# One weight load of 1 MB issued as sixteen loads of eight partitions each

## The chip, the cores and the metric

The kernel runs on one core of one Trainium2 chip. The metric is the device time of one execution in microseconds (us). A core has a matrix engine (PE, with weight loads PEld), a vector engine (DVE), a scalar engine (ACT), GpSimd (POOL), a sequencer that here only issues transfers (SP), and 16 DMA engines that carry the transfers of all of them.

## The reference

Two blocks follow one another on a sequence of 256 tokens with 1024 features, all in float32.

The first block is attention over chosen keys beside a short convolution, and then a feed-forward layer made of 16,384 small experts. Each token has 8 heads; each head picks 16 experts; and the layer is the sum over all these picks:

```
u_sel = peer_u[expert]
a = jax.nn.gelu(jnp.einsum('bqhkd,bqd->bqhk', u_sel, hb))
v_sel = peer_v[expert]
return jnp.einsum('bqhk,bqhkd->bqd', g * a, v_sel)
```

The second block has two layers, each with its own weights `w_in_2`, `w_branch_attn_2`, `w_branch_gmlp_2` and `w_out_2`: a projection into nine parts, sliding-window attention, a gated unit, two branch projections, an output projection, and a layer norm.

## The kernel before, in words

The instructions of each engine are written out by hand, with semaphores between them. Four parts of it matter here.

**The expert stage.** Tokens stand in 128 partitions, in two tiles. For tile, head and pick (2 x 8 x 16 = 256 times) POOL issues one indirect transfer, a gather (L901): each of 128 partitions gets the 8 KB row of its own expert (1024 features of `peer_u`, 1024 of `peer_v`), 1 MB in all. Gather n goes to slot n modulo 12; six slots lie in the tile `rows`, six in `low_pairs`. Before it issues gather n, POOL waits until PE has used gather n - 12 (`pair_used`). When a gather has landed, DVE takes the dot product (L2063), ACT the GELU (L1140), DVE the weight (L2070), ACT builds a diagonal matrix (L1145), and PE adds the pick to the sum with eight products (L1569). ACT and PE do this for four picks at a time.

**The weight ring.** Weights come in units of 128 partitions x 8 KB (1 MB). The tile `wring` has four places. Units 0 to 30 belong to the first block, unit 31 (`N1`) is the first of 2 x 27 units of the second block's layers. Each is split by ACT (`layer_hi`, L704) and DVE (`layer_lo`, L710) into a rounded part and a rest before PE uses it.

**The order of SP.** SP issues all weight loads from one queue. After the last load of the first block it waits for the expert scores (L807, L808), and then runs the loop of L813 to L845. For unit 31 nothing more is waited for: it is issued at once, while the expert stage is under way. For the next one (L816, L817) SP waits until gather 253 has landed, and for the one after that until gather 255, the last, has landed (L820). Each load adds 16 to the semaphore of its ring place, `w_loaded[s]`, and the readers wait for 16 times the number of loads of that place (`w_wait`, L606).

**The first use.** ACT reads unit 31 within the last group of picks: `layer_hi(act, 0, 0)` at L1153, after a pick among the last, and pieces 1 to 3 soon after it.

The transfers of SP and ACT are of the kind `hardware_dynamic` in the profile, those of POOL `software_dynamic`.

Of the kernel before, what the change touches and what calls it, by code (L numbers as in the profile page):

```python
# [22 lines left out]
P = 128  # L23
# [16 lines left out]
RING = 4  # L40
# [60 lines left out]
N1, N2 = len(UNITS_1), len(UNITS_2)  # L101
# [29 lines left out]
def own_group(n):  # L131

    return [n in group for group in OWN_GROUPS].index(True)
# [17 lines left out]
def ada_place(n):  # L151

    if n < 2 * KC:
        return n % FIRST_RING, n // FIRST_RING, n - FIRST_RING if n >= FIRST_RING else None
    place, turn = (n - 2 * KC) % ADA_RING, (n - 2 * KC) // ADA_RING
    return place, 2 * KC // FIRST_RING + turn, n - (ADA_RING if turn else FIRST_RING)


def raw_turn(n):

    return n - sum(own < n for own in OWN_UNITS)
# [87 lines left out]
def use(name, i=0):  # L249

    return [n for n, z in enumerate(USES) if z.name == name][i]
# [64 lines left out]
def build(nc, a, out):  # L316
    ctx = ExitStack()
    with ctx:
        def sb(name, shape, dt=F32):
            return ctx.enter_context(nc.sbuf_tensor(name, shape, dt))  # L320

        def sem(name):
            return ctx.enter_context(nc.semaphore(name))


        wring = sb("wring", [P, RING, WUNIT])
# [63 lines left out]
        spread = ytok.rearrange("p n f -> p (n f)")[0:NT * HEADS, :]  # L390
# [16 lines left out]
        w2 = Area(work[:, :])  # L407
# [81 lines left out]
        w_loaded, own_loaded = [sem(f"w_loaded{s}") for s in range(RING)], [sem(f"own_loaded{s}") for s in range(len(OWN_GROUPS))]  # L489
# [46 lines left out]
            sem("routed"), sem("gate_exp"), sem("dotted"), sem("dots_act"), sem("weighted"), sem("diag_ready"))  # L536
        pair_loaded = [sem(f"pair_loaded{s}") for s in range(SLOTS)]
        pair_used = sem("pair_used")
        x_ready = sem("x_ready")
        bias_iota, bias_lin, bias_ready = sem("bias_iota"), sem("bias_lin"), sem("bias_ready")  # L540
        vn_ready, vn_std, vn_stat = sem("vn_ready"), sem("vn_std"), sem("vn_stat")
# [23 lines left out]
        def chunk_out(m, width=T):  # L565
            b, j, _, _ = SEATS_1[m]
            z = aux[:, 3 + b, :] if b < BATCH else pj[:, b % 2, :]
            return z[:, j * T:j * T + width]
# [23 lines left out]
        def bank_free(pe, m):  # L592
# [3 lines left out]
            if j == 0 and b >= BATCH + 2:  # L596
                last = SEATS_1[first - 1][2]
                who = OWN_1[last - 1]
                pe.wait_ge({"a": taken_act, "d": taken_dve}[who], OWN_1[:last].count(who))

        def w_wait(eng, n):

            if n in OWN_UNITS:
                eng.wait_ge(own_loaded[own_group(n)], 16 * len(OWN_GROUPS[own_group(n)]))
            else:
                eng.wait_ge(w_loaded[raw_turn(n) % RING], 16 * (raw_turn(n) // RING + 1))  # L606

        def w_slot(n):
            width, chunks = UNITS_1[n][2:] if n < N1 else (256, KC)
# [19 lines left out]
        def split_hi(act, n):  # L629

            if PIECES_1[n].column == 0:
                w_wait(act, PIECES_1[n].unit)

            before = [k for k, z in enumerate(PIECES_1) if z.place <= PIECES_1[n].place - PRING]
            if before:
                act.wait_ge(proj, DONE_1[before[-1]])
            nc.scalar.copy(parts(n)[0], piece_of_unit(n)).then_inc(w_hi, 1)
# [23 lines left out]
        def wait_emptied(eng, l, u):  # L661

            who = USES[u].owner
            eng.wait_ge(emptied[who], l * EMPTIES[who] + sum(z.owner == who for z in USES[:u + 1]))
# [26 lines left out]
        def layer_hi(act, l, *pieces):  # L691

            for p in pieces:
                unit = N1 + l * N2 + p // 2
                if p % 2 == 0:
                    w_wait(act, unit)
                r = ring_place(l, p)
                if r is not None and r >= PRING:
                    was, q = RING_ORDER[r - PRING]
                    act.wait_ge(steps, was * STEPS + PIECE_DONE[q])  # L700
                if r is None:
                    act.wait_ge(steps, l * STEPS + FILLED[use("bg", 3)])
                    act.wait_ge(y_split, l * 2 + 2)
                nc.scalar.copy(layer_part("hi", l, p), layer_raw(l, p)).then_inc(w_hi, 1)  # L704
# [7 lines left out]
        def wait_lo(eng, l, p):  # L712

            eng.wait_ge(w_lo["d"], LO_1.count("d") + SPLIT_ORDER.index((l, p)) + 1)
# [45 lines left out]
        def _(sp):  # L760
# [3 lines left out]
            def load_ada(n):  # L764
                place, turn, was = ada_place(n)
                if was is not None:
                    sp.wait_ge(ada_used, was + 1)
                sp.dma_start(ada[:, place, :], a["w_ada"][ada_column(n)]).then_inc(ada_loaded[place], 16)
# [41 lines left out]
            def load_rows(dst, name, l, done):  # L810
                sp.dma_start(dst, a[name][l:l + 1].partition_broadcast(P).rearrange("p o d -> p (o d)")).then_inc(done, 16)

            for l in range(LAYERS):  # L813
                for n in range(N2):
                    unit = N1 + l * N2 + n
                    if l == 0 and n == 1:  # L816
                        sp.wait_ge(pair_loaded[(LAST_PICK - 2) % SLOTS], 16 * ((LAST_PICK - 2) // SLOTS + 1))  # L817
                    if l == 0 and n == 2:
                        load_rows(vg_rows.rearrange("p l f -> p (l f)"), "vg_rows", 0, vg_rows_loaded)
                        sp.wait_ge(pair_loaded[LAST_PICK % SLOTS], 16 * (LAST_PICK // SLOTS + 1))  # L820
                    if l == 0 and n == 4:
                        sp.wait_ge(routed, NT * EXPERT_HEADS)
                        sp.wait_ge(gate_exp, NT * EXPERT_HEADS)
                        load_rows(late_rows, "late_rows", 0, late_rows_loaded)
                    if l == 0 and n == 6:
                        load_rows(brow.rearrange("p l n -> p (l n)"), "brow", 0, brow_loaded)
                    if n == 10:
                        if l == 0:
                            sp.wait_ge(x0_turned, 2 * NT)
                        else:  # L830
                            wait_emptied(sp, l - 1, use("gg", 3))
                        load_rows(gate_rows, "gate_rows", l, gate_rows_loaded)
                    if n == 17:
                        sp.wait_ge(att2["summed"], l * NT + NT)
                        load_rows(norm_rows, "norm_rows", l, norm_rows_loaded)
                        if l + 1 < LAYERS:
                            sp.wait_ge(x0_taken, 2 * NT)
                            sp.wait_ge(vn_ready, l * NT + NT)
                            load_rows(late_rows, "late_rows", l + 1, late_rows_loaded)
                    if unit - RING >= N1:  # L840
                        was, q = divmod(unit - RING - N1, N2)
                        wait_lo(sp, was, 2 * q)
                        wait_lo(sp, was, 2 * q + 1)
                    s = raw_turn(unit) % RING
                    sp.dma_start(wring[:, s, :], a["w2"][l, n]).then_inc(w_loaded[s], 16)  # L845
            for t in range(NT):
                for c in range(2):
                    sp.wait_ge(x_normed, (LAYERS - 1) * 2 * NT + 2 * t + c + 1)
# [424 lines left out]
        def _(pe):  # L1273
# [83 lines left out]
            def first_products(k, n):  # L1357

                pe.wait_ge(h_ready, k + 1)
                w_wait(pe, n)  # L1360
                w, m = w_slot(n), 2 * n
                for j in range(1 if n == 2 else 2):
                    ins = mm(chunk_out(m + j), w[:, k, j * P:(j + 1) * P], hT[:, k, :], start=(k == 0 and j == 0), stop=(k == KC - 1),  # L1363
                             skip_group_check=True)
                    if k == KC - 1 and n < 2:
                        ins.then_inc(proj, 1)
                if n == 2:
                    for t in range(NT):
                        ins = mm(chunk_out(m + 1)[:, t * HEADS:(t + 1) * HEADS], hT[:, k, tile_of(t)], w[:, k, P:P + HEADS], start=False, stop=(k == KC - 1),
                                 skip_group_check=True)  # L1370
                    if k == KC - 1:
                        ins.then_inc(proj, 2)
# [377 lines left out]
        def _(dve):  # L1750
# [3 lines left out]
            def ada_dots(lo, hi):  # L1754

                for n in range(lo, hi):
                    place, turn, _ = ada_place(n)
                    dve.wait_ge(ada_loaded[place], 16 * (turn + 1))
                    tile = ada[:, place, :]
                    v.tensor_tensor_reduce(tile, tile, cbc, 1.0, 0.0, ALU.mult, ALU.add,  # L1760
                                           mod[:, ada_column(n):ada_column(n) + 1]).then_inc(ada_used, 1)
# [622 lines left out]
```

## Time and profile before

| what | value |
|---|---|
| median of three runs | 1176.72 us (1174.97 to 1177.11) |
| the profiled execution, its own time | 1175.45 us |
| its span | 1173.5 us |
| PE, PEld, DVE, ACT, POOL busy | 90%, 84%, 71%, 37%, 23% of the span |
| moved by DMA | 390.35 MB, 333 GB/s over the span |
| of it gathers | 268.45 MB |

The span is cut into 40 slices of 29.3 us in the page's second part. The expert stage takes slices 6 to 28; there the row of GB/s stands at 419 to 422 almost without a break, and after it at 160 to 230.

### The profile page before, as it was taken

How to read it: one execution, taken by the hardware profiler on the slowest of the kernel's cores; microseconds unless marked ns; L12 is line 12 of the kernel's file. 1: busy time of each engine (PE TensorE's matmuls, PEld its weight loads, DVE VectorE, ACT ScalarE, POOL GpSimd, SP SyncE). 2: the span in 40 equal slices, each digit the busy share in tenths (PEclk: the TensorE clock that was granted, in tenths of full speed). 3: DMA queues.
4: the chain of work that ended last, by engine and by line, in shares of the span. 5: the costliest groups of instructions: out<-in, count | busy, mean ns of one | idle time of the engine just before them, and what ended most of it. 6: DMA issues, size and time to landing. Idle time of an engine off the chain costs nothing.

```text
span 1173.5 us, 18891 instructions
## 1 busy us (share of the span) xinstructions
PE 1052.4 (90%) x7587; PEld 982.2 (84%) x7587; DVE 836.9 (71%) x1801; ACT 432.9 (37%) x913; POOL 269.0 (23%) x289
## 2 busy tenths in 40 slices
PE   8999997999999888887777878778999999999997
PEld 6999986998899878887777878778899888898885
DVE  6999987568566667666776766656765868775776
ACT  3646832123212221222122122212557554476452
POOL 2001004334334333333333333434000000300000
PEclk9999998999999998899898998999999999999999
DMA  9986858999999999999999999999855655455540
GB/s 371 406 330 224 350 189 350 419 421 419 422 419 421 420 421 421 420 421 420 421 420 420 421 421 421 421 421 421 348 185 177 232 198 180 157 202 180 193 166 36
DMA packets 59576, 390.35 MB, mean 333 GB/s; under 512 B 6881, under 2 KB 7905, under 8 KB 15714
## 3 DMA queue, kind: packets, MB, share of 16 engines
q0 software_dynamic: 36864, 268.45, 55.1%
q1 hardware_dynamic: 21152, 120.10, 27.5%
q8 instruction: 60, 0.98, 0.3%
q10 hardware_dynamic: 1474, 0.60, 0.2%
q14 instruction: 26, 0.21, 0.0%
HBM read 388.08 MB, written 1.05 MB: 332 GB/s over the span
## 4 chain that ended last, share of the span: by engine, by line
PE 60%; DMA 26%; DVE 7%; ACT 4%; issue 1%; SPq 0%; DVEq 0%; ACTq 0%
DMA rows<-in_peer_uv,work 25%; PE aux L1569 22%; PE pj L1612 5%; PE pj L1614 5%; PE pj L1613 5%; PE pj L1289 5%; PE pj L1290 5%; PE pj L1291 5%; PE aux L1548 4%; DVE rows L2063 2%; DMA rows<-in_w_ada 1%; PE aux L1363 1%; ACT work L1145 1%; ACT rows L1013 1%; PE aux L1428 1%
## 5 line engine op out<-in xcount | busy, mean ns | idle before, releaser
L1569 PE MATMUL aux<-work,rows 128*128 128x128 f32 x2080 | 262.9, 291 | 70.7 <-ACT work L1145 70.7
L1569 PEld LDWEIGHTS aux<-work,rows 128*128 128x128 f32 x2080 | 256.1, 206 | 78.2 <-ACT work L1145 78.0
L1569 PE MATMUL aux<-work,low_pairs 128*128 128x128 f32 x2016 | 239.7, 280 | 30.5 <-ACT work L1145 30.3
L1569 PEld LDWEIGHTS aux<-work,low_pairs 128*128 128x128 f32 x2016 | 234.6, 196 | 34.1 <-ACT work L1145 34.1
L901 POOL DMA_INDIRECT rows<-in_peer_uv,work x130 | 122.4, 942 | 296.0 <-PE aux L1569 229.6
L710 DVE TENSOR_TENSOR wlo<-wring,whi 128x1024 fp32r<-128x1024 f32 x100 | 121.0, 1235 | 77.7 <-ACT whi L704 77.1
L901 POOL DMA_INDIRECT low_pairs<-in_peer_uv,work x126 | 118.2, 938 | 160.5 <-PE aux L1569 155.8
L1289 PE MATMUL pj<-xh,whi 128*128 128x256 f32 x512 | 146.4, 286 | 0.2
L1140 ACT ACTIVATE work<-work 128x4 f32<-128x4 f32 (+2 forms) x71 | 14.7, 207 | 357.1 <-DVE work L2063 357.1
L1290 PE MATMUL pj<-xl,whi 128*128 128x256 f32 x512 | 144.8, 283 | 0.0
L1291 PE MATMUL pj<-xh,wlo 128*128 128x256 f32 x512 | 144.8, 283 | 0.0
L2063 DVE CUSTOM_DVE_ANT_0 low_pairs<-low_pairs,aux 128x1024 f32<-128x1024 f32 x64 | 77.6, 1220 | 54.2 <-DMA low_pairs<-in_peer_uv,work 54.1
L704 ACT CAST whi<-wring 128x1024 fp32r<-128x1024 f32 x100 | 102.2, 1050 | 24.7 <-PE pj L1614 23.3
L2063 DVE CUSTOM_DVE_ANT_0 rows<-rows,aux 128x1024 f32<-128x1024 f32 x64 | 77.0, 1218 | 39.3 <-DMA rows<-in_peer_uv,work 39.2
L1289 PEld LDWEIGHTS pj<-xh,whi 128*128 128x128 f32 x512 | 98.1, 192 | 2.6 <-issue 1.8
L1290 PEld LDWEIGHTS pj<-xl,whi 128*128 128x128 f32 x512 | 98.2, 192 | 0.0
L1291 PEld LDWEIGHTS pj<-xh,wlo 128*128 128x128 f32 x512 | 98.2, 192 | 0.0
L1145 ACT ACTIVATE work<-ident,work 128x128 f32<-128x128 f32 x256 | 82.6, 390 | 21.5 <-DVE work L2070 21.5
L2063 DVE CUSTOM_DVE_ANT_0 rows<-rows,pj 128x1024 f32<-128x1024 f32 x66 | 78.1, 1217 | 16.7 <-DMA rows<-in_peer_uv,work 16.3
L2063 DVE CUSTOM_DVE_ANT_0 low_pairs<-low_pairs,pj 128x1024 f32<-128x1024 f32 x62 | 73.6, 1218 | 22.5 <-DMA low_pairs<-in_peer_uv,work 22.2
L1612 PE MATMUL pj<-whi,xh 128*128 128x512 f32 x192 | 76.0, 396 | 1.7 <-DVE xl L2077 1.3
L1614 PE MATMUL pj<-wlo,xh 128*128 128x512 f32 x192 | 74.9, 390 | 0.0
(288 smaller groups left out, 1464.4 us busy)
## 6 DMA issues: line engine op xcount, KB each, us to landing
wring<-in_w SPq DMA_DIRECT2D x76, 1024.0 KB, 4.8
rows<-in_w_ada SPq DMA_DIRECT2D x46, 512.0 KB, 9.2
rows<-in_w SPq DMA_DIRECT2D x3, 1024.0 KB, 11.2
rows<-in_peer_uv,work POOLq DMA_INDIRECT x130, 17.3
work<-in_late_rows SPq DMA_DIRECT2D x2, 1024.0 KB, 7.6
xT<-in_gate_rows SPq DMA_DIRECT2D x2, 1024.0 KB, 7.5
rows<-in_norm_rows SPq DMA_DIRECT2D x2, 1024.0 KB, 7.5
low_pairs<-in_peer_uv,work POOLq DMA_INDIRECT x126, 17.9
```

The source lines that it names most:

```text
L704: nc.scalar.copy(layer_part("hi", l, p), layer_raw(l, p)).then_inc(w_hi, 1)
L710: dve.tensor_tensor(layer_part("lo", l, p), layer_raw(l, p), full(layer_part("hi", l, p)), ALU.subtract).then_inc(w_lo["d"], 1)
L901: pool.indirect_dma_start(out=pair(n), out_offset=None, in_=a["peer_uv"], in_offset=bass.IndirectOffsetOnAxis(ap=expert[g % EXPERTS][:, j: ...
L1145: nc.scalar.activation(diag[:, j, :], ident[:, :], ACT.Copy, scale=weight[g % 2][:, j:j + 1]).then_inc(diag_ready, 1)
L1289: mm(o, w[0], x[0], start=start, stop=False, skip_group_check=skip)
L1290: mm(o, w[0], x[1], start=False, stop=False, skip_group_check=skip)
L1291: return mm(o, w[1], x[0], start=False, stop=stop, skip_group_check=skip)
L1569: ins = mm(peer_sum[t][:, c * P:(c + 1) * P], pair(n)[:, D + c * P:D + (c + 1) * P], diag[:, n % PICKS, :], start=(n % (EXPERT_HEADS * PIC ...
L1612: mm(bank(u), hi[:, k, ts], w_hi_[:, j, :], start=(k == 0), stop=False)
L1613: mm(bank(u), lo[:, k, ts], w_hi_[:, j, :], start=False, stop=False)
L1614: ins = mm(bank(u), hi[:, k, ts], w_lo_[:, j, :], start=False, stop=(k == last))
L2063: v.tensor_tensor_reduce(row, row, h2_tok[g // EXPERT_HEADS], 1.0, 0.0, ALU.mult, ALU.add, dots[g % 2][:, j:j + 1]).then_inc(dotted, 1)
```

## The change

Unit 31 is loaded by sixteen transfers in place of one. Transfer i carries partitions 8i to 8i + 7 (`SPREAD_ROWS` = 8), 64 KB, and adds 16 to a semaphore of its own, `spread_loaded`. The readers of unit 31 wait for 256 there. The later loads of the same ring place count one load fewer. All other loads are as before, and so are their order and the waits ahead of them.

```
+SPREAD_UNIT, SPREAD_ROWS = N1, 8
...
+        def loads_till(n):
+
+            spread = raw_turn(n) % RING == raw_turn(SPREAD_UNIT) % RING and raw_turn(n) > raw_turn(SPREAD_UNIT)
+            return raw_turn(n) // RING + 1 - spread
+
         def w_wait(eng, n):
...
+            elif n == SPREAD_UNIT:
+                eng.wait_ge(spread_loaded, 16 * (P // SPREAD_ROWS))
             else:
-                eng.wait_ge(w_loaded[raw_turn(n) % RING], 16 * (raw_turn(n) // RING + 1))
+                eng.wait_ge(w_loaded[raw_turn(n) % RING], 16 * loads_till(n))
...
                     s = raw_turn(unit) % RING
-                    sp.dma_start(wring[:, s, :], a["w2"][l, n]).then_inc(w_loaded[s], 16)
+                    if unit == SPREAD_UNIT:
+                        for at in range(0, P, SPREAD_ROWS):
+                            rows_ = slice(at, at + SPREAD_ROWS)
+                            sp.dma_start(wring[rows_, s, :], a["w2"][l, n][rows_, :]).then_inc(spread_loaded, 16)
+                    else:
+                        sp.dma_start(wring[:, s, :], a["w2"][l, n]).then_inc(w_loaded[s], 16)
```

## Rows read from the trace of the kernel before

**Rows 1.** Busy time by stretch: us, engines' busy (instructions), PEclk, DMA share, GB/s.
```profile
177.00:190.00 13.00, 12.44 (x62) 10.84 (x63) 5.11 (x23) 3.61 (x8) 7.51 (x7) 1.00 0.76 286
...
230.00:393.00 163.00, 152.05 (x1224) 146.43 (x1222) 110.91 (x282) 40.16 (x108) 62.42 (x67) 1.00 1.01 420
393.00:403.00 10.00, 8.53 (x77) 8.49 (x77) 8.75 (x29) 6.42 (x15) 3.97 (x5) 1.00 1.01 420
403.00:813.00 410.00, 329.06 (x2637) 321.64 (x2636) 273.35 (x656) 87.01 (x239) 153.31 (x166) 0.93 1.01 421
```

**Rows 2.** Chain that ended last, 751 to 835 us: start, us, what.
```profile
751.34 20.84 DMA rows<-in_peer_uv,work
...
774.42 7.42 PE aux L1569 x64
781.85 0.26 issue
782.11 19.91 DMA rows<-in_peer_uv,work
...
811.94 21.13 DMA rows<-in_peer_uv,work
833.07 0.02 issue
833.09 1.22 DVE rows L2063
```

**Rows 3.** SP's waits, 400 to 850 us: us in total, times, longest.
```profile
SPq L845 <- DMA rows<-in_peer_uv,work: 438.5, 2, 433.4
```

**Rows 4.** SP in order of time: start, us, instruction.
```profile
393.13 0.33 SPq L845 DMA_DIRECT2D wring<-in_w  x1
...
826.84 0.33 SPq L845 DMA_DIRECT2D wring<-in_w  x1
827.21 0.74 SPq L811 DMA_DIRECT2D pq<-in_vg_rows  x1
833.09 0.80 SPq L845 DMA_DIRECT2D wring<-in_w  x2
```

**Rows 5.** Instructions on wring, 820 to 850 us: ns min/median/max, first and last start.
```profile
L704 ACT CAST whi<-wring x7: 1028/1034/1055, 822.2 to 849.3; 128x1024 fp32r<-128x1024 f32 x7
```

**Rows 6.** DMA issues of 388 to 394 us: KB each, us to landing.
```profile
wring<-in_w SPq DMA_DIRECT2D x1, 1024.0 KB, 10.3
```

**Rows 7.** DMA queues of the whole span: packets, MB, share of 16 engines.
```profile
q0 software_dynamic: 36864, 268.45, 55.1%
...
q10 hardware_dynamic: 1474, 0.60, 0.2%
```

**Rows 8.** DMA issues of ACT in the whole span: KB each, us to landing.
```profile
wsT<-in_wsT ACTq DMA_DIRECT2D x1, 512.0 KB, 20.0
...
cols<-in_cols ACTq DMA_DIRECT2D x1, 45.0 KB, 5.4
lcol<-in_lcol ACTq DMA_DIRECT2D x1, 18.0 KB, 23.0
rows<-in_c ACTq DMA_DIRECT2D x1, 4.0 KB
sink<-in_sink ACTq DMA_DIRECT2D x1, 8.0 KB, 21.4
```

**Rows 9.** Busy time by stretch at the end of the expert stage, columns as above.
```profile
820.00:822.00 2.00, 1.86 (x17) 1.67 (x16) 1.65 (x5) 0.69 (x3) 0.00 (x0) 1.00 0.96 397
822.00:824.00 2.00, 2.00 (x21) 2.00 (x20) 1.73 (x4) 1.71 (x4) 0.00 (x0) 1.00 0.73 307
824.00:826.00 2.00, 2.00 (x21) 2.00 (x20) 1.92 (x3) 0.13 (x2) 0.00 (x0) 1.00 0.56 233
```

**Rows 10.** DMA queues, 393 to 827 us: packets, MB, share of 16 engines.
```profile
q8 instruction: 22, 0.36, 0.3%
q14 instruction: 10, 0.08, 0.0%
```

More of the change, by code:

```diff
@@ L538, in build @@
         pair_used = sem("pair_used")
+        spread_loaded = sem("spread_loaded")
         x_ready = sem("x_ready")
```

## The prediction

> **What bounds the kernel now.** I read the table of stretches first, then the chain of waits, then SP's own waits and issues, and last the DMA queues. The change touches one load, so the question is what runs beside it and whether that is on the path to the end.
>
> The load is issued at 393.13 us [rows 4]. In the stretches around it all sixteen DMA engines are full: a share of 1.01 at 420 GB/s from 230 to 393 us, during the load, and from 403 to 813 us at 421 GB/s, while PE is busy for 329 of 410 us (80%) and DVE for 67% [rows 1]. No compute engine is full there, the transfers are. At the start of the expert stage that was not yet so, 0.76 from 177 to 190 us [rows 1]. The chain of waits says the same: it goes round a loop of a gather that takes 20 to 21 us to land, some 2.4 us on DVE and ACT, 7.42 us of PE (64 products, eight picks), 0.26 us, and the next gather [rows 2]. From landing to landing (772.18 us, from 751.34 + 20.84, to 802.02, from 782.11 + 19.91) that is 29.8 us for the twelve gathers of the twelve slots, 2.49 us each; and 1.05 MB at 421 GB/s is 2.49 us. So the DMA engines set the pace of this stage, and a microsecond of extra work on the engine that is last is a microsecond at its end.
>
> The end of the stage is on the path as well. The last gather lands at 833.07 us; DVE takes it at 833.09 [rows 2] and SP issues the next weight units at 833.09 [rows 4], so the second block moves with it.
>
> **The change part by part.** The sums are made in the profiled execution (1175.45 us, span 1173.5 us, so 1.95 us lie around it); it is 1.27 us below the median of 1176.72 us, and I add the change to the median.
>
> *Issue on SP.* Fifteen more issues of 0.33 us; two in a row take 0.80 us [rows 4], so about 0.4 us each, 6 us in all. Behind them in SP's queue stands a wait of 433.4 us for gather 253 [rows 3]. Cost nothing; it would cost from a 434th microsecond on.
>
> *Wait of the readers.* The unit is first read at 822.2 us [rows 5], 429 us after its issue; it landed after 10.3 us [rows 6]. Even a landing four times slower is hidden. The new semaphore and the count of the later loads cost nothing: the number of wait instructions is the same.
>
> *Bytes.* The same 1 MB. As one transfer over 16 engines it is 64 KB for each, eight rows of 8 KB. An engine moves 421 / 16 = 26.3 GB/s, so a row takes 0.311 us and the load takes 2.49 us from every engine. That cost is in the time before.
>
> *Which engines.* No row shows a plain transfer of eight partitions. The nearest is the one of a single row: ACT's load of `c`, 4 KB [rows 8]. Queue q10 holds ACT's transfers, 1474 packets [rows 7]. Three loads of 128 partitions (`cols`, `lcol`, `sink`) are 384 packets, `wsT` is 8 pieces x 128 = 1024, and `c` as one piece is 1: 1409. The other 65 are 4 x 16 + 1, a closing packet for each engine that took part: sixteen for each of the four wide loads, a single one for `c`. The gathers agree: 36864 packets are 256 x (128 + 16) [rows 7]. So a transfer of one row ran on one engine, and I take it that one of eight rows runs on eight. If these are the same eight each time, each gets 16 rows, 4.98 us, and the other eight none. Bounds: nothing (if the sixteen transfers take turns over all engines) and 8 x 0.311 = +2.49 us on eight engines. I take +2.49, because it is nearest to the row of `c`.
>
> The Trainium skill says so outright in "DMA: Bandwidth & Descriptors", section "Why a DMA increments its semaphore by 16 and not by 1": the number of engines is the largest up to 16 that divides the outer sizes, and for transfers issued by SP or ACT they are the lowest-numbered ones. By it eight rows go to the same eight engines each time; the one closing packet of `c` agrees, and which eight they are no row here shows.
>
> *Whether the eight get in each other's way.* In the wide load and in every gather each engine has its own eight partitions. In a small transfer eight engines write to eight neighbouring partitions at the same moment. If neighbours share a way into the memory, a packet there takes longer, and its engine can't go on with its gather in that time. No row shows this. Lower bound: 0.311 us for a row as ever, nothing more. Upper bound: four engines at one place from beginning to end, so a row takes 4 x 0.311 and each of sixteen transfers costs 3 x 0.311 = 0.93 us more, 14.9 us in all. Between packets of the small transfers each engine has a gather packet, which goes to its own place, so the engines fall out of step and the four seldom meet in full. I take two at a time: 16 x 0.311 = +4.98 us. Both ends are kept for the range.
>
> *Slack.* The engines are not level. The last gather is issued at 811.94 us and its last part lands at 833.07 [rows 2], yet the share of the DMA engines falls to 0.96, 0.73 and 0.56 from 820 to 826 us [rows 9]: some have finished all their gathers while others have seven microseconds to go. What else the engines carry can unlevel them: 22 + 10 packets of instructions fall between 393 and 827 us [rows 10], and not evenly, I suppose. A lag on an engine that is ahead is free as far as its lead goes. Up to 826 us the idle time is 2 x (0.04 + 0.27 + 0.44) = 1.5 us per engine on the mean; the bounds are 0 (the last engine is one of the eight) and about 12 us (the first to finish, 821 against 833). I take -1.5.
>
> *The sum.* 2.49 + 4.98 - 1.5 = +6.0 us: 1181.4 us for the profiled execution, 1182.7 us for the median.
>
> **The rivals.**
>
> *In step.* The four engines at one place stay together for all sixteen transfers: 2.49 + 14.9 = +17.4, with the slack +15.9 us, 1192.6 us. For it: SP issues every 0.4 us, so all eight engines find their row at the same time. Against it: the gather packets between them, as above. The Trainium skill, "SBUF — State Buffer", section "Door 1: The DMA port swizzle (why `[64,N]` ≈ `[32,N]`)", speaks for it: four neighbouring partitions lie on one of 16 ports, so eight reach two, and a load into one port ran at 27.6 GB/s. As an estimate from that page, 64 KB over two ports would be 1.2 us and all sixteen 19 us, against 5 us without sharing. No run here shows it so far.
>
> *Eight engines and no more.* The rows don't hinder one another, and the slowest engine is one of the eight: +2.49 us, 1179.2 us. For it the row of `c`; against it only that neighbours have never been written together in this trace.
>
> *No change.* The sixteen transfers take turns over all engines, or the eight have a lead of over 2.5 us at the end: 0 to +1 us, 1176.7 us. For it: the share of 0.56 at 824 to 826 us says that many engines have such a lead. Against it: with the hold-up the lead would have to be 7.5 us.
>
> *Faster.* The slowest engine, the one that lands last at 833.07 us, is among the eight that get nothing of unit 31. It is then relieved of eight rows, -2.49 us, 1174.2 us. This decides only if the eight that get the rows lag by less than their lead, so with a hold-up of nearly nothing. For it: it is one half or the other; against it: as the gain grows to the full 2.49 us, another engine becomes the last.
>
> That the change does not do what it says would need the unit to land after 822 us or a reader to wait elsewhere; the 429 us above leave no room for it.
>
> **How the numbers follow.** Hold-up of about the assumed size (+3.5 to +10 us): 0.45. In step (+10 to +20): 0.15. Eight engines alone (+1 to +3.5): 0.15. No change: 0.17. Faster: 0.08. The bound of what can be told from no change is 0.2%, 2.35 us. Slower by more than it are the first two and about half of the third, 0.67; faster by more than it is a part of the last, and I give it 0.08 with what a measurement scatters; within it the rest, 0.25. The range goes from 1175.5 us, which holds the cases of no change and leaves out most of the faster one, to 1190 us, which leaves out the upper part of the case in step.
>
> **What would show it.** In the profile after, SP issues sixteen transfers from about 393 us on, about 0.4 us apart. Queue q1 has 16 x (8 + 8) = 256 packets for the unit in place of 144, 112 more; 16 x (8 + 16) = 384, so 240 more, would say that every small transfer closes on all engines and that they are spread wider. The share of the DMA engines, or the GB/s, falls below 421 within some 20 us after 393 us if there is a hold-up: 6 us of lost time on eight engines is a dip to about 300 GB/s over 10 us. It stays level where the engines only carry more. The stage's last gather lands at 839 us in place of 833, and the second block keeps its length of 340 us. From 820 us to the last landing there is more idle time, because the other eight engines finish about 2.5 us earlier against the rest. The forecast is wrong if the last landing moves by less than 3 us, or if it moves and the second block gives it back.

## The result, and the profile after

The kernel after takes 1191.63 us (four runs, 1191.26 to 1192.53), the kernel before 1175.93 us (four runs). The ratio is 1.0135, with a 95% interval of 1.0123 to 1.0147: slower by some 15.9 us. The forecast was 1182.7 us, in a range of 1175.5 to 1190. The span of the profiled execution grew from 1173.5 to 1189.7 us, by 16.2 us.

The table of stretches around the load, kernel after (us, busy time of PE, PEld, DVE, ACT and POOL with their instructions, granted PE clock, DMA share, GB/s):

```profile
230.00:393.00 163.00, 151.54 (x1219) 145.88 (x1217) 110.53 (x280) 40.64 (x109) 62.49 (x67) 1.00 1.01 421
393.00:398.00 5.00, 4.04 (x36) 4.04 (x37) 4.71 (x9) 4.46 (x10) 0.94 (x1) 1.00 1.02 357
398.00:403.00 5.00, 5.00 (x48) 5.00 (x47) 3.50 (x20) 1.49 (x5) 2.81 (x3) 1.00 1.03 228
403.00:408.00 5.00, 5.00 (x47) 5.00 (x46) 0.54 (x2) 0.00 (x0) 2.00 (x3) 1.00 1.00 215
408.00:413.00 5.00, 1.40 (x13) 1.20 (x11) 1.23 (x2) 0.00 (x0) 1.76 (x2) 1.00 1.04 202
413.00:418.00 5.00, 0.00 (x0) 0.00 (x0) 0.13 (x1) 0.00 (x0) 0.00 (x0) 0.55 1.04 205
418.00:423.00 5.00, 0.00 (x0) 0.00 (x0) 1.10 (x2) 0.00 (x0) 0.00 (x0) 0.50 1.03 200
423.00:428.00 5.00, 0.89 (x4) 0.89 (x5) 2.76 (x9) 1.48 (x5) 0.00 (x0) 0.50 0.94 352
...
453.00:813.00 360.00, 283.29 (x2297) 276.43 (x2296) 242.88 (x595) 77.22 (x212) 134.63 (x144) 0.95 1.01 420
```

Before, this stretch was level at 420 GB/s [rows 1]. Now the same sixteen engines are as busy as ever (share 1.00 to 1.04) and move half as much, for close to 30 us. PE runs out of picks and stands still from 413 to 423 us. After 428 us all is as before. The bytes that were not moved can be added up: (64 + 193 + 206 + 219 + 216 + 221 + 69) GB/s x 5 us are 5.9 MB, which is 14.1 us at 421 GB/s. I call this the lost throughput of a run; below it is worked out for each kernel in the same way. It is a loss of all sixteen engines together: eight engines that stood still for 14 us would lose half of it.

The chain that ended last, kernel after (start, us, what), around the load and at the end of the stage:

```profile
391.61 0.26 issue
391.87 33.00 DMA rows<-in_peer_uv,work
...
427.11 9.04 PE aux L1585 x64
...
436.41 19.24 DMA rows<-in_peer_uv,work
...
828.13 21.07 DMA rows<-in_peer_uv,work
```

The same gather, and the one that follows it, in the chain of the kernel before:

```profile
392.42 16.16 DMA rows<-in_peer_uv,work
...
418.50 20.83 DMA rows<-in_peer_uv,work
```

It takes 33.0 us to land in place of 16.16. The eight picks on PE behind it take 9.04 us in place of 7.42 [rows 2], because PE starts them at a granted clock of 0.50 (1.2 GHz) after its idle time. That adds nothing: the next gather of the chain lands at 455.65 us (436.41 + 19.24) against 439.33 before (418.50 + 20.83), 16.3 us late, as the one before it (424.87 against 408.58). The last gather lands at 849.20 us (828.13 + 21.07) in place of 833.07 [rows 2]: 16.1 us. From there to the end of the span it is 340.5 us, before 340.4. So the whole loss lies in these 30 us, and the second block gave nothing back and lost nothing.

SP's issues, and the queues from 393 to 425 us (packets, MB, share of 16 engines), kernel after:

```profile
392.59 5.41 SPq L859 DMA_DIRECT2D wring<-in_w  x16
```

```profile
q0 software_dynamic: 887, 6.46, 87.3%
q1 hardware_dynamic: 256, 1.05, 13.8%
```

In the kernel before the same 32 us have these rows:

```profile
q0 software_dynamic: 1698, 12.35, 92.9%
q1 hardware_dynamic: 144, 1.05, 7.9%
```

The unit takes 256 packets, 16 x (8 + 8), and not 16 x (8 + 16): a transfer of eight rows runs on eight engines. Issue takes 0.34 us each (5.41 / 16) and nobody waits for it; behind it SP waits 445.0 us for gather 253. What changed is the time of a packet: those of the gathers went from 92.9% x 512 / 1698 = 0.28 us to 87.3% x 512 / 887 = 0.50 us on the mean (closing packets included). The trace also records each packet by itself, though not its engine. A gather packet of 8 KB takes 0.309 to 0.321 us as a rule; in the kernel after, 98% of the 523 that start between 398 and 423 us take over 0.335 us, 0.644 in the median. Eight engines that nothing held would have brought at least half of these packets, in the usual time. So the gathers of all sixteen engines are held up, and not only those of the eight that bring the small rows.

### The profile page after: what moved, and what is told of

The parts are those of the page before. It is cut to its first block, busy times and chain, and to the rows that moved or that the text cites. A ratio compares the mean times of both kernels' runs of the same rounds, so it can differ in the third digit from the quotient of the medians.

```text
span 1189.7 us, 18906 instructions
## 1 busy us (share of the span) xinstructions
PE 1047.9 (88%) x7587; PEld 977.4 (82%) x7587; DVE 836.8 (70%) x1801; ACT 433.0 (36%) x913; POOL 270.1 (23%) x289
## 4 chain that ended last, share of the span: by engine, by line
PE 59%; DMA 28%; DVE 7%; ACT 4%; issue 1%; SPq 0%; DVEq 0%; ACTq 0%
DMA rows<-in_peer_uv,work 26%; PE aux L1585 21%; PE pj L1628 5%; PE pj L1630 5%; PE pj L1629 5%; PE pj L1305 5%; PE pj L1306 4%; PE pj L1307 4%; PE aux L1564 4%; DVE rows L2079 2%; DMA rows<-in_w_ada 1%; PE aux L1379 1%; ACT work L1161 1%; ACT rows L1029 1%; PE aux L1444 1%
## 5 line engine op out<-in xcount | busy, mean ns | idle before, releaser
L1585 PE MATMUL aux<-work,rows 128*128 128x128 f32 x2080 | 256.0, 286 | 88.2 <-ACT work L1161 88.2
L1585 PEld LDWEIGHTS aux<-work,rows 128*128 128x128 f32 x2080 | 249.0, 201 | 95.9 <-ACT work L1161 95.7
L1585 PE MATMUL aux<-work,low_pairs 128*128 128x128 f32 x2016 | 242.5, 282 | 33.4 <-ACT work L1161 33.3
L1585 PEld LDWEIGHTS aux<-work,low_pairs 128*128 128x128 f32 x2016 | 237.4, 198 | 37.1 <-ACT work L1161 37.1
```

The source lines that it names most:

```text
L1585: ins = mm(peer_sum[t][:, c * P:(c + 1) * P], pair(n)[:, D + c * P:D + (c + 1) * P], diag[:, n % PICKS, :], start=(n % (EXPERT_HEADS * PIC ...
```

## The experiments

The theories at the start: *shared places* (neighbouring partitions share a way into the memory, and their rows wait for one another; such a way in, with the partitions behind it, is called a place below), *number of transfers* (each small one costs something, wherever it writes), *half the engines*, and shared places on the *source* side. All kernels are measured against the kernel before.

### Every fourth partition

```
-                        for at in range(0, P, SPREAD_ROWS):
-                            rows_ = slice(at, at + SPREAD_ROWS)
-                            sp.dma_start(...)
+                        for at in range(0, P, 4 * SPREAD_ROWS):
+                            for j in range(4):
+                                rows_ = slice(at + j, at + 4 * SPREAD_ROWS, 4)
+                                sp.dma_start(...)
```

> Still sixteen transfers of eight rows on eight engines, but each takes every fourth partition (0, 4, ... 28, then 1, 5, ... 29, and so on), in the source as in the ring. Shared places (eight neighbours have two ways into the memory, the rows wait for one another): no two of the eight meet, the dip to 205 GB/s for some 30 us goes away, and what is left is the eight extra rows on eight engines, -2.5 to +2.5 us against before: 1173.5 to 1178.5 us. Number of transfers (each small transfer costs the DMA engines about a microsecond, wherever it writes): 1191 us as with the change. Eight engines carry the load of sixteen and that alone: at most +2.5 us, and it could not have made +16 in the first place.

Measured: ratio 1.0049 (1.0035 to 1.0062), +5.8 us. Number, size and engine count of the transfers are those of the change, and nearly two thirds of its cost are gone. But it is more than the 2.5 us that shared places allowed. The stretches of this kernel show where the rest is:

```profile
393.00:398.00 5.00, 3.52 (x32) 3.36 (x31) 4.04 (x9) 4.46 (x10) 1.42 (x2) 1.00 1.01 421
398.00:403.00 5.00, 5.00 (x48) 5.00 (x47) 4.69 (x22) 1.97 (x6) 2.54 (x3) 1.00 1.02 419
403.00:408.00 5.00, 5.00 (x47) 5.00 (x46) 2.39 (x6) 0.00 (x0) 2.13 (x3) 1.00 1.01 323
408.00:413.00 5.00, 2.07 (x19) 1.88 (x17) 1.47 (x4) 0.21 (x1) 1.88 (x2) 1.00 1.03 306
413.00:418.00 5.00, 4.53 (x26) 4.53 (x27) 3.84 (x12) 1.28 (x4) 0.94 (x1) 0.68 1.00 388
```

The first half (partitions 0 to 63) loses nothing, the second half falls to 306 GB/s: (98 + 115 + 33) x 5 / 421 = 2.9 us lost, and with 2.5 us for eight rows more on eight engines 5.4 us.

### The upper half first

The same with `for at in (64, 96, 0, 32)`.

> The run of every fourth partition lost nothing while partitions 0 to 63 were written and fell to some 310 GB/s for ten microseconds while 64 to 127 were. Here the upper half goes first. If the upper partitions are the places of the eight engines that get no row of the small transfers (guests and owners share them), the dip comes at once, from about 395 us, and the second part is level: 1180.5 us again. If the dip came from having many transfers queued, it stays in the second part.

Measured: ratio 1.0050 (1.0035 to 1.0066), +5.9 us. The dip moved to the front:

```profile
393.00:398.00 5.00, 4.29 (x38) 4.29 (x39) 4.95 (x10) 4.25 (x8) 1.11 (x2) 1.00 1.03 387
398.00:403.00 5.00, 5.00 (x47) 5.00 (x47) 3.80 (x19) 1.48 (x5) 2.63 (x3) 1.00 1.02 295
403.00:408.00 5.00, 5.00 (x48) 5.00 (x47) 1.23 (x2) 0.00 (x0) 2.25 (x3) 1.00 1.00 328
408.00:413.00 5.00, 1.14 (x11) 0.95 (x9) 1.71 (x3) 0.00 (x0) 1.50 (x2) 0.98 1.01 416
```

So it belongs to partitions 64 to 127 and not to the time or to a full queue. Lost in these four stretches: (34 + 126 + 93 + 5) x 5 / 421 = 3.1 us. The simplest reading: the same eight engines bring all sixteen transfers, their gathers write the lower half, and in the upper half they meet the gathers of the other eight. That engine and half belong together is inferred from this dip, no row names an engine.

### Sixteen neighbours, thirty-two neighbours

`SPREAD_ROWS` = 16 and 32: eight and four transfers, sixteen engines in each.

> Eight transfers of sixteen neighbouring partitions. All sixteen engines take part, one row each. Shared places: sixteen rows have four ways in, so four engines still meet in each; eight transfers cost 3 x 0.311 us each on all engines, +7.5 us, about 1183.5 us. Engine count (half the engines): nothing is left, 1176 us. Number of transfers: half of +16, 1184 us, which only the run by columns tells from the first.

> Four transfers of 32 neighbouring partitions, two rows for each of sixteen engines. Thirty-two neighbours have eight places, so two engines meet in each: 4 transfers x 2 rows x 0.311 us = +2.5 us, and up to twice that with the owners of the places, 1177.5 to 1180 us. If the price went by the number of transfers and the rows in each alone, a quarter of the change's: +4 us, 1179 us. If sixteen engines in use were enough to be rid of it: 1175 us.

Measured: 1.0074 (1.0060 to 1.0087), +8.7 us, and 1.0033 (1.0023 to 1.0044), +3.9 us. With sixteen engines in use the loss is still there, so *half the engines* is not the cause of the dip (it is that of the 2.5 us of uneven rows, see below). In the sixteen-row kernel the rate is as low as in the change, for half as long:

```profile
398.00:403.00 5.00, 5.00 (x48) 5.00 (x47) 3.12 (x19) 1.60 (x6) 2.81 (x3) 1.00 1.03 202
403.00:408.00 5.00, 5.00 (x48) 5.00 (x47) 1.23 (x2) 0.00 (x0) 1.87 (x2) 1.00 1.07 220
```

### By columns

```
+                        for at in range(0, WUNIT, WUNIT // 16):
+                            part_ = slice(at, at + WUNIT // 16)
+                            sp.dma_start(wring[:, s, part_], a["w2"][l, n][:, part_]).then_inc(spread_loaded, 16)
```

> Sixteen transfers as well, but each over all 128 partitions, 512 bytes of each row. Shared places: every engine writes its own partitions as in the gathers, no dip; 0 to +2 us for the shorter pieces, 1176 to 1178 us. Number of transfers: 1191 us.

Measured: 1.0013 (1.0004 to 1.0022), +1.5 us. Sixteen transfers of 64 KB cost next to nothing if each covers all partitions, even cut into pieces of 512 bytes. SP takes 21.3 us to issue these sixteen, against 5.4 in the change, so they come in more thinly; the run apart in time, below, shows that thinness alone does not help, and the run with sixteen more rows has sixteen small transfers and no dip. *Number of transfers* falls. The lowest rate from 398 to 428 us is this:

```profile
413.00:418.00 5.00, 5.00 (x47) 5.00 (x46) 2.79 (x5) 0.00 (x0) 2.81 (x3) 1.00 1.00 399
```

### Source rows apart

```
+                            rows_, block_ = slice(at, at + SPREAD_ROWS), at // 32 * 32 + at // SPREAD_ROWS % 4
+                            from_ = slice(block_, block_ + 4 * SPREAD_ROWS - 3, 4)
+                            sp.dma_start(wring[rows_, s, :], a["w2"][l, n][from_, :]).then_inc(spread_loaded, 16)
```

> Sixteen transfers of eight neighbouring partitions of the ring, as in the change, but the eight rows are read four rows apart in DRAM (unit 31 is then loaded with its rows in another order, so what follows is computed from other weights). Shared places on the side of the ring: 1191 us, as with the change. Shared places on the side of DRAM (eight rows that follow one another are read from one 64 KB piece): 1174 to 1179 us.

Measured: 1.0152 (1.0136 to 1.0169), +17.9 us, the same as the change within the intervals. Reading the rows apart does not help by itself; every fourth partition, where they are written apart as well, does. The *source side* falls.

### Each transfer by itself, beside the gathers

```
+                            rows_, gather = slice(at, at + SPREAD_ROWS), 86 + 3 * (at // SPREAD_ROWS)
+                            if at:
+                                sp.wait_ge(pair_loaded[gather % SLOTS], 16 * (gather // SLOTS + 1))
```

> The change's sixteen transfers of eight neighbours, but each is issued three gathers (7.5 us) after the one before, so they never meet one another. Hold-up inside each transfer: every one still holds its eight engines for 3 x 0.311 us or more, and the loss stays near +15 us, 1190 us, in sixteen small dips. Hold-up by the queue of transfers (they overtake one another or pile up): most of it goes, 1178 us.

Measured: 1.0149 (1.0134 to 1.0165), +17.5 us. The transfers do not need one another to cost what they cost. The dip is only thinner and longer (the first of the sixteen falls into the first line):

```profile
396.00:401.00 5.00, 4.37 (x39) 4.37 (x40) 4.87 (x10) 4.31 (x9) 1.19 (x2) 1.00 1.02 354
401.00:413.00 12.00, 12.00 (x110) 12.00 (x109) 10.09 (x35) 2.91 (x10) 6.09 (x7) 1.00 1.01 420
413.00:533.00 120.00, 90.81 (x684) 88.90 (x683) 70.91 (x169) 23.77 (x62) 39.61 (x43) 0.89 1.01 377
```

The packets show who pays. Within some 3 us of each of the sixteen transfers, 33 to 48 gather packets take over 0.335 us (the longest of each 0.86 to 1.23 us), while 91 of the 128 rows of the small transfers stay below 0.335. What these gather packets take beyond the usual time is 11 to 17 us of engine time per transfer, 14.2 on the mean, 0.89 us for each of sixteen engines. Eight engines held for 3 x 0.311 us would be 7.5.

### The same loads with the DMA engines idle

The kernel before, and behind the last weight load 1 MB five times into a free place of the ring, each after the last has landed (`load_alone` issues its list and waits for it):

```
+            load_alone(0, [slice(0, P)])
+            load_alone(1, [slice(at, at + 8) for at in range(0, P, 8)])
+            load_alone(2, [slice(0, P)])
+            load_alone(3, [slice(at + j, at + 32, 4) for at in range(0, P, 32) for j in range(4)])
+            load_alone(4, [slice(0, P)])
```

> The kernel before, and near its end, when the DMA engines have nothing else to do, SP loads 1 MB five times into a free place of the ring, each load after the last has landed: wide, sixteen of eight neighbours, wide, sixteen of every fourth, wide. Read from SP's times, not from the kernel's. Shared places: wide 4.8 us; neighbours 16 x 4 x 0.311 = 20 us and 2 us of latency; every fourth 10.7 us of issue at 0.67 us each and 2 us of latency (16 x 0.311 = 5 us of rows fit below it). Without a hold-up of neighbours: 16 x 0.34 = 5.4 us of issue and 2 us of latency, some 8 us.

SP's issues of this kernel (start, us, what); a load has landed when the first issue of the next one starts. Some that lie between are left out:

```profile
1140.72 0.33 SPq L852 DMA_DIRECT2D wring<-in_w  x1
...
1145.46 0.67 SPq L852 DMA_DIRECT2D wring<-in_w  x2
...
1160.71 0.36 SPq L852 DMA_DIRECT2D wring<-in_w  x1
...
1165.79 4.74 SPq L852 DMA_DIRECT2D wring<-in_w  x7
...
1178.35 0.36 SPq L852 DMA_DIRECT2D wring<-in_w  x1
```

Wide: 4.74 us (1140.72 to 1145.46) and 5.08 us (1160.71 to 1165.79). Neighbours: 15.25 us, of which their issue at 0.34 us each is 5.4. So the hold-up is there without any gather. The packets say how large it is: a row of the wide load takes 0.309 us in the median, the rows of the neighbours 0.47 to 0.92, half of them between 0.77 and 0.89. The eight rows of a transfer start together, and the next eight start when they end; all 128 take 13.5 us, 0.84 for a transfer. The expectation of four rows in turn, 4 x 0.311 = 1.24 us and 20 us in all, was too high, and not because transfers overlap: four rows at one place take some 0.9 us together. From 1152 to 1160 us the rate is 71 GB/s, against 262 from 1141 to 1145 in the wide load:

```profile
1141.00:1145.00 4.00, 4.00 (x21) 3.07 (x20) 3.72 (x5) 2.28 (x3) 0.00 (x0) 1.00 0.80 262
1152.00:1160.00 8.00, 8.00 (x38) 6.59 (x37) 6.77 (x12) 0.88 (x2) 0.00 (x0) 1.00 0.44 71
```

Every fourth: 12.56 us (1165.79 to 1178.35). Its issue accounts for most of it, since a strided transfer takes SP 0.67 us to issue (10.7 us for sixteen) against 0.34. Its rows take 0.31 to 0.61 us, so this part of the run does not show them free of any hold-up. Each of these times is from one execution.

### Sixteen more rows on eight engines

```
+                        for again in range(2):
+                            for at in range(0, 64, 32):
+                                for j in range(4):
+                                    rows_ = slice(at + j, at + 32, 4)
+                                    sp.dma_start(wring[rows_, s, :], a["w2"][l, n][rows_, :]).then_inc(more_loaded, 16)
+                            sp.wait_ge(more_loaded, 128 * (again + 1))
                     sp.dma_start(wring[:, s, :], a["w2"][l, n]).then_inc(w_loaded[s], 16)
```

> The kernel before, and ahead of unit 31 sixteen small transfers (every fourth partition of 0 to 63, twice over): 16 rows more for each of eight engines and nothing for the other eight, in places where the first run saw no dip. It tells on which side the slowest engine is. Among the eight: +5.0 us, 1180.2 us. Among the other eight: these eight lag by 5 us less their lead, 0 to +2 us, 1175 to 1177 us.

Measured: 1.0048 (1.0034 to 1.0061), +5.6 us, and no dip at all:

```profile
398.00:403.00 5.00, 5.00 (x48) 5.00 (x46) 4.69 (x22) 1.75 (x6) 2.76 (x3) 1.00 1.02 419
...
413.00:418.00 5.00, 4.38 (x40) 4.18 (x38) 1.73 (x4) 0.00 (x0) 2.95 (x4) 1.00 1.01 418
```

1 MB more at 421 GB/s would be 2.5 us if all engines carried it alike. It costs twice that, the sixteen rows in full, so the engine that is last is one of the eight. The interval, 4.0 to 7.2 us, leaves out the other answer (0 to +2 us).

### Every second and every sixteenth partition

As every fourth, with a step of 2 (`at` in steps of 16), and with `rows_ = slice(at, P, 16)` for `at` from 0 to 15.

> Sixteen transfers of eight rows, each over every second partition (0, 2, ... 14, then 1, 3, ... 15). Eight neighbours put four rows on each of two places, every second partition puts two rows on each of four. If the price goes by how many meet in one place: between every fourth (+5.4 us) and neighbours (+15.9 us): the part above +2.5 us falls to a third (one other in place of three), and the owner of the place comes on top, about +9 us, 1184.5 us. If only true neighbours are in each other's way: 1180.5 us, as every fourth.

> Sixteen transfers of eight rows sixteen partitions apart (0, 16, ... 112, then 1, 17, ... 113). If places are groups of four neighbours and nothing more, all eight rows are in different places: +2.5 to +5.5 us, 1178 to 1181 us. If partition p shares its place with p + 32 (and the upper half has places of its own), the eight rows have four places, two rows in each: the same as every second, about 1184.5 us.

Measured: 1.0086 (1.0064 to 1.0109), +10.1 us, and 1.0105 (1.0083 to 1.0128), +12.3 us. A step of 16 is dearer than a step of 4, though its rows lie farther apart. So a place is not just four neighbours: of partitions 0, 16, ... 112 some must share one too. Which ones this run alone does not say; rows 16 apart, such as 0 and 16, are also among those of every fourth. Half of the rows of either kernel lie in partitions 64 to 127, so the meeting with the gathers there, as in every fourth, does not make the difference. The lowest rates of the two kernels, every second first:

```profile
408.00:413.00 5.00, 1.22 (x11) 1.03 (x10) 0.19 (x1) 0.00 (x0) 1.59 (x2) 0.88 0.98 234
```

```profile
413.00:418.00 5.00, 0.00 (x0) 0.00 (x0) 1.22 (x2) 0.00 (x0) 0.10 (x1) 0.83 1.02 247
```

By the Trainium skill, "SBUF — State Buffer", section "Door 1: The DMA port swizzle (why `[64,N]` ≈ `[32,N]`)", partitions 0 to 3 and 32 to 35 are one port and 64 up are other ports. By it steps of 1, 2, 4 and 16 give eight rows 2, 4, 8 and 4 ports; measured are +15.9, +10.1, +5.8 and +12.3 us, in that order, and the intervals of the two cases of four ports overlap. The trace agrees with the order; that it is 32 which makes the rows meet rests on the map.

### All of them in one sum

Lost throughput is taken from the stretches of 5 us from 393 to 428 us (for the run apart in time from 396 to 543 us, 380 GB/s), against 421 GB/s. "Uneven" is 8 x 0.311 us where eight engines carry sixteen rows each (twice that where they carry sixteen more), 0 where all sixteen carry alike.

| kernel | lost, us | uneven, us | sum | measured, us (from the ratio) |
|---|---|---|---|---|
| the change | 14.1 | 2.5 | 16.6 | +15.9 |
| source rows apart | 12.7 | 2.5 | 15.2 | +17.9 |
| apart in time | 14.3 | 2.5 | 16.8 | +17.5 |
| every sixteenth | 8.4 | 2.5 | 10.9 | +12.3 |
| every second | 7.5 | 2.5 | 10.0 | +10.1 |
| sixteen neighbours | 7.3 | 0 | 7.3 | +8.7 |
| upper half first | 3.0 | 2.5 | 5.5 | +5.9 |
| every fourth | 2.9 | 2.5 | 5.4 | +5.8 |
| sixteen more rows | 0 | 5.0 | 5.0 | +5.6 |
| thirty-two neighbours | 4.0 | 0 | 4.0 | +3.9 |
| by columns | 0.8 | 0 | 0.8 | +1.5 |

The order of the sums follows the times but for the three at the top, whose intervals overlap. The intervals are 1 to 3 us to each side, so the table bears out the two terms together, and not each figure to a tenth. In nine of the eleven kernels the measured time is above the sum, by 0.1 to 2.7 us, so something small may be missing from it.

No kernel here beats the kernel before. The one load over all partitions is already the form with no dip and, by its packets, with eight rows for every engine; what it costs is its 2.49 us of all engines.

## Why the prediction was wrong, point by point

*What bounds.* Right: the loss arises in the transfers beside the gathers, and arrives at the end one to one (16.3 us at the landing at 424.87 us against 408.58 before, 16.1 us at the last landing, 16.2 us in the span).

*Issue and readers.* Right: hidden, as worked out.

*Which engines.* Right: eight, by the 256 packets. The term of +2.49 us stands, and the run with sixteen more rows gives it its full size.

*Whether the eight get in each other's way.* This step failed: "I take two at a time: 16 x 0.311 = +4.98 us." What the runs leave for this term is 15.9 - 2.5 = 13.4 us, with the slack at nothing. Two things were wrong in it. First, the argument for the lower value was that the engines fall out of step because they do gathers in between. The run apart in time shows why that does not help: a single transfer of eight neighbours, with nothing of its kind near it, costs 17.5 / 16 = 1.1 us at the end, its uneven row included. Second, it let a crowded place hold only the eight engines that bring the rows. The packets show all sixteen held, 14.1 us of lost throughput for the whole set; the upper bound of 14.9 us on eight engines would have lost half of that, 7.5 us. So that 13.4 lies near 14.9 does not confirm the bound. Its own picture, four rows that take 4 x 0.311 us, did not come true where it could be seen alone: there a row took some 0.9 us and a transfer 0.84. The prediction's estimate from the Trainium skill, "SBUF — State Buffer", section "Door 1: The DMA port swizzle (why `[64,N]` ≈ `[32,N]`)", 1.2 us for 64 KB over two ports and 19 us for all, is above these 0.84 and 13.5 us; the measurement decides.

*Slack.* Failed too, and in the same direction: "I take -1.5." It was read from the mean lead of all engines [rows 9]. What counts is the lead of the last of the eight, and sixteen more rows on them cost 5.6 us (4.0 to 7.2), the full 5.0, so it has none that shows. Both errors together, 13.4 - 4.98 and 1.5, are the 9.9 us between +6.0 and +15.9; that they add up is no proof, since 13.4 is itself what was left over.

*The rivals.* The one called "in step" came out, +15.9 us, but the exact agreement is luck: it counts a slack of 1.5 us that is not there, and holds eight engines where all sixteen were held. Without the slack it would have said +17.4. It had a chance of 0.15. "No change" and "faster" needed a hold-up of nearly nothing.

*What was to show it.* The 256 packets and the unchanged 340 us of the second block came as forecast; the last gather landed at 849.2 us and not at 839. The dip was there, deeper and longer (200 to 228 GB/s for 25 us) than the 300 GB/s over 10 us that +6.0 would have made.

## What to carry to other kernels

Where transfers set the pace, look at which partitions each of them writes. A load that covers all 128 partitions can be cut along its columns for +1.5 us, but the same megabyte cut along its partitions cost +15.9 us, though it was needed 429 us later: a load that is never waited for can still slow all others. And where a cost lies between far bounds because several requests may meet, ask whether one transfer alone makes them meet, and whether the traffic beside it is held as well; here it did and was, and the lower choice was wrong.

## What the runs showed of the hardware that was not expected

The hold-up reaches engines that bring no row of the small transfer. In the change 98% of the gather packets from 398 to 423 us are long, and in the run apart in time up to 17 or 18 long ones are under way at once around each small transfer, which takes all sixteen engines (records of packets that follow one another overlap a little). In sixteen neighbours, where all engines take part, the rate falls to 202 GB/s; in the change, where eight do, to 200. Where nothing is crowded nothing is held: in every fourth partition one of 263 gather packets is long while partitions 0 to 63 are written, and 96% are while 64 to 127 are. Why a few crowded places hold all engines is left open.

A strided set of partitions doubles the issue time on SP, 0.67 us (10.78 / 16 in every fourth partition) against 0.34, with the same eight rows of 8 KB.
